# A three-block network on one core: the opening's first two weight units take the raw input, and their results are scaled afterwards

## The reference, cut to what matters

```python
def _rmsnorm(a, gain):
    af = a.astype(jnp.float32)
    af = af * lax.rsqrt(jnp.mean(af * af, axis=-1, keepdims=True) + EPS)
    return (af * gain.astype(jnp.float32)).astype(a.dtype)
...
    (q_sb, k_sb, v_sb, q_sp, k_sp, v_sp, q_ix, k_ix, w_ix,
     q_df, k_df, v_df, g_sb, g_sp, g_df) = _split_cols(u @ w_in)
...
        dots = jnp.einsum('bqjd,bkd->bqjk', qib.astype(jnp.float32), k_ixf)
        score = jnp.einsum('bqj,bqjk->bqk', wb.astype(jnp.float32), jax.nn.relu(dots))
        score = jnp.where((key_pos[None, :] <= qpos[:, None])[None], score, NEG_INF)
        _, sel = lax.top_k(score, top_k)
```

## Time and profile before

| | us |
|---|---|
| median of 3 runs | 2647.53 |
| lowest and highest of the runs | 2644.81, 2650.80 |
| the profiled execution | 2655.39 |
| its span, from the first instruction to the last | 2653.6 |

### The profile page before, as it was taken

The page is one execution under the profiler, slowest core; times in us unless marked ns, Lnnn a source line. Parts: engine busy times, 40 slices in busy tenths (PEclk is TensorE's granted clock), DMA queues, the critical chain, the costliest instruction groups (busy, mean ns, idle before and its releaser), DMA issues.

```text
span 2653.6 us, 36450 instructions
## 1 busy us (share of the span) xinstructions
PE 2548.8 (96%) x14788; PEld 2074.2 (78%) x14788; DVE 1481.2 (56%) x2440; ACT 1029.1 (39%) x1817; POOL 300.9 (11%) x213
## 2 busy tenths in 40 slices
PE   8889999999999999999999999999999999999998
PEld 6678898998998877766577777878866687788886
DVE  4987654554445457476547887454744644433444
ACT  4465454443223253235542223255333333322323
POOL 0143210012222010000012222020000000000001
PEclk9999999999999999998999999999999999999999
DMA  4211122223232341520035664332221132233332
GB/s 170 89 49 56 49 71 59 76 83 96 91 93 90 95 143 48 174 72 2 1 103 183 206 192 134 95 111 80 88 72 48 56 92 91 81 94 95 96 95 72
DMA packets 76980, 244.83 MB, mean 92 GB/s; under 512 B 12708, under 2 KB 18213, under 8 KB 76558
## 3 DMA queue, kind: packets, MB, share of 16 engines
q1 hardware_dynamic: 69470, 215.72, 26.3%
q10 hardware_dynamic: 7344, 26.77, 3.0%
HBM read 238.25 MB, written 6.90 MB: 92 GB/s over the span
## 4 chain that ended last, share of the span: by engine, by line
PE 66%; DVE 9%; ACT 3%; issue 2%; POOL 0%; DMA 0%; SPq 0%; ACTq 0%; DVEq 0%
PE ps L595 55%; DVE wl L379 2%; PE ps L2784 2%; ACT wh L367 1%; PE ps L1810 1%; PE ps L3477 1%; PE ps L1827 1%; PE ps L1838 1%; DVE xl L676 1%; DVE arena L1064 1%; DVE arena L3147 1%; PE ps L769 1%; PE ps L3461 1%; PE ps L1665 0%; PE ps L1545 0%
## 5 line engine op out<-in xcount | busy, mean ns | idle before, releaser
L595 PE MATMUL ps<-xh,wh 128*128 128x512 f32 (+1 forms) x2728 | 1006.7, 383 | 22.8 <-DVE xl L676 7.5
L595 PE MATMUL ps<-xl,wh 128*128 128x512 f32 (+1 forms) x2728 | 988.6, 377 | 0.0
L595 PE MATMUL ps<-xh,wl 128*128 128x512 f32 (+1 forms) x2728 | 984.4, 375 | 0.0
L379 DVE TENSOR_TENSOR wl<-ring,wh 128x1024 fp32r<-128x1024 f32 x374 | 472.8, 1264 | 593.8 <-ACT wh L367 593.0
L367 ACT ACTIVATE wh<-ring 128x1024 fp32r<-128x1024 f32 x372 | 393.2, 1057 | 938.9 <-PE ps L595 838.6
L595 PEld LDWEIGHTS ps<-xh,wh 128*128 128x128 f32 x2728 | 500.1, 189 | 151.3 <-issue 41.1
L595 PEld LDWEIGHTS ps<-xh,wl 128*128 128x128 f32 x2728 | 499.7, 189 | 97.8
L595 PEld LDWEIGHTS ps<-xl,wh 128*128 128x128 f32 x2728 | 498.3, 189 | 97.4 <-issue 5.5
L2060 PE MATMUL ps<-xh,wh 128*128 128x264 f32 (+1 forms) x816 | 254.2, 311 | 5.3 <-DVE xl L433 3.8
L759 POOL TENSOR_TENSOR arena<-arena 128x512 f32<-128x512 f32 (+1 forms) x35 | 60.2, 1726 | 1626.9 <-ACT arena L744 1626.9
L2060 PE MATMUL ps<-xl,wh 128*128 128x264 f32 (+1 forms) x816 | 233.3, 286 | 0.0
(11 more groups left out here) (388 smaller groups left out, 2571.1 us busy)
## 6 DMA issues: line engine op xcount, KB each, us to landing
ring<-in_weights SPq DMA_DIRECT2D x374, 512.0 KB, 3.6
arena<-in_w_ada ACTq DMA_DIRECT2D x48, 512.0 KB, 4.5
arena<-in_cmp_w SPq DMA_DIRECT2D x2, 2048.0 KB
strip_copies<-strip_scratch SPq DMA_DIRECT2D x8, 327.5 KB, 6.5
arena<-strip_copies SPq DMA_DIRECT2D x8, 264.0 KB, 4.0
out_features<-arena SPq DMA_DIRECT2D x8, 256.0 KB, 2.1
token_scratch<-arena SPq DMA_DIRECT2D x3, 512.0 KB, 6.8
arena<-token_scratch SPq DMA_DIRECT2D x12, 128.0 KB, 4.0
```

The costliest lines, as they stand in the source:

```text
L379: dve.tensor_tensor(flat(self.wl[:, s % 2]), flat(self.ring[:, s % RING]), flat(self.wh[:, s % 2]).bitcast(F32), ALU.subtract).then_inc(se ...
L595: last = pe.matmul(self.place(u, e), w[:, k, :], x[:, k, o:o + m], start=(k == 0 and i == 0), stop=(k == self.chunks - 1 and i == 2))
```

## The change

Units 0 and 1 now take the input times the gain, without the root. The new stages are:

- `raw`, an `Inputs` with gains: ACT rounds gain times chunk to `xh` straight from `h` (L616), DVE makes `xl` from `h`, gain and `xh` (L624).
- `RawSums`: ACT squares (L733); POOL adds squares 1 to 5 up (four additions, L746); PE sums square 0, the POOL's total, squares 6 and 7 with `ones` (L757), four pairs of products where there were eight; ACT makes the root (L737, L738).
- `Renormed`: the input is made once more, with gain and root (DVE L711, ACT L694, then the remainder L686, by POOL for chunks 2, 4 and 6, by DVE for the others), with three buffers where there were two. Unit 2 is the first to take it. Each chunk's `xh` waits until unit 1 has used the raw one (`raw_left`).
- `Scaled`: POOL multiplies the results of units 0 and 1 by the root (L775).

Unit 1 runs two chunks behind unit 0. The index keys become unit 0, the index queries units 1 and 2. ACT's queue now issues three of the four input transfers, and SP's issues the first unit's weights ahead of the fourth. The small work of `Prepare` moves from ahead of and within unit 2 to unit 3.

```diff
-    units = [pack_units(c) for c in [col[6], np.concatenate(col[7:9], 1)] + col[0:3] + col[9:12] + col[3:6]]
+    units = [pack_units(c) for c in [np.concatenate(col[7:9], 1), col[6]] + col[0:3] + col[9:12] + col[3:6]]
...
+class Renormed(Stage):
...
+        self.by_pool = (2, 4, 6)
...
+    def part(self, eng, k):
+        eng.wait_ge(self.hi.sem, self.hi.at(k + 1))
+        return eng.tensor_tensor(self.core.xl[:, k, 0:self.T], self.out[:, k % 3], self.core.xh[:, k, 0:self.T].bitcast(F32),
+                                 ALU.subtract)
...
+    def pool(self, pool):
+        for k in self.by_pool:
+            yield self.at + self.d * (k + 1) + 0.05
+            self.part(pool, k).then_inc(self.lo_pool.sem, 1)
+
+    def vector(self, dve):
+        for k in range(NC + 2):
+            yield self.at + self.d * k
+            if k == 0:
+                dve.wait_ge(self.sums.root.sem, self.sums.root.at(1))
+            if k >= 2 and k - 2 not in self.by_pool:
+                self.part(dve, k - 2).then_inc(self.lo.sem, 1)
+            if k < NC:
+                if k >= 3:
+                    self.split(dve, k - 3)
+                dve.scalar_tensor_tensor(out=self.out[:, k % 3], in0=self.tiles[k], scalar=self.gains[k], in1=self.sums.r,
+                                         op0=ALU.mult, op1=ALU.mult).then_inc(self.made.sem, 1)
...
+class RawSums(Stage):
...
+    def pool(self, pool):
+        for n in range(1, 5):
+            yield self.times[n + 1] + 0.1
+            pool.wait_ge(self.squared.sem, self.squared.at(n + 2))
+            if n > 1:
+                pool.wait_ge(self.added.sem, self.added.at(n - 1))
+            pool.tensor_tensor(self.acc, self.sq[:, 1] if n == 1 else self.acc, self.sq[:, (n + 1) % 4], ALU.add).then_inc(
+                self.added.sem, 1)
...
+class Scaled(Stage):
...
+    def pool(self, pool):
+        for n, a in enumerate(self.tiles):
+            yield self.at + 0.4 * n
+            pool.wait_ge(self.sums.root.sem, self.sums.root.at(1))
+            self.ready(pool, n)
+            pool.tensor_tensor(a, a, self.sums.r, ALU.mult).then_inc(self.done.sem, 1)
...
-        walk = [(u, e, k) for k in range(NC) for u in range(together) for e in range(2)]
+        walk, together, lag = [], 2 if self.x else 0, 2
+        for k in range(NC + lag if self.x else 0):
+            walk += [(0, e, k) for e in range(2) if k < NC] + [(1, e, k - lag) for e in range(2) if k >= lag]
...
-        for i in (1, 3):
-            self.load(sp, i)
+        yield -3.0
+        self.load(sp, 3)
...
-        for i in (0, 2):
+        for i in (0, 1, 2):
             self.load(act, i)
...
+    raw = Inputs(core, tokens_in, None, T, gains, landed, [-0.7, -0.66, -0.6, -0.54, -0.48, -0.44, -0.42, -0.4])
+    sums = RawSums(core, [-0.68, -0.64, -0.62, -0.58, -0.56, -0.52, -0.5, -0.46], tokens_in, landed, T, values + 5120, core.area(norm_tmp, T))
+    raw_left = core.take("raw_left", NC - 1)
+    core.chunk_used = [(raw_left.sem, raw_left.at(k + 1)) for k in range(NC - 1)] + [(core.used, 2)]
+    renormed = Renormed(core, tokens_in, 1.6, 0.125, T, sums, gains, norm_tmp + T)
```

More of the change, by code:

```diff
@@ L2874, in leave @@
         return act.activation(P1[:, u, o:o + n], got, ACT.Copy, scale=0.125 if u in (SB_Q, SB_Q + 1) else 1.0)
-    proj = Halved(core, N1, 0, halves(T), leave, x)
+    proj = Halved(core, N1, 0, halves(T), leave, (raw, renormed))
+    proj.raw_left = raw_left
+    scaled = Scaled(core, 2.2, [P1[:, u, :] for u in range(2)],
+                    lambda pool, u: pool.wait_ge(proj.free.sem, proj.free.at(2 * u + 2)), sums)
     whole = halves(T)
```

196 lines of the change are left out of this document (95 added, 101 removed).

## The result

The changed kernel takes **2658.28 us** (median of 7 runs, 2653.32 to 2662.75), beside 2647.53 for the kernel before (seven runs of each): a ratio of 1.0038 with a 95% interval of 1.0026 to 1.0050, so 6.9 to 13.2 us slower. The forecast was 2653.9, within 2645.0 to 2659.5: the median lies inside the range, 4.4 above the forecast.

A forecast was written before the change was run, and what follows sets the result against it. The opening's turning of the index weights was taken to set the end: root at 26.9, last chunk at 43.9, turning at 50.3 instead of 43.84. That 6.4 on the median 2647.53 gave 2653.9 us, range 2645.0 to 2659.5.

The forecast's parts named there:

- The first weights: Opening: the first unit's weights, issued at about 1.7, land at 7.7, with 7.4 and 10.07 as ends.
- Stops in the first part: Opening up to chunk 2: POOL's four additions each hold DVE 1.0, so chunk 2 is ready at 17.9 instead of 13.9.
- The root: Summed squares on TensorE, then logarithm, exponential and handing over: the root is there at 26.9, before it was 17.2.
- the low spell of 1.5: TensorE ahead of the root: one spell at 1.2 GHz, 15 products each 0.10 slower, adding 1.5 us.
- The second part: Root to last remainder: DVE's work 12.4 with waits, POOL's five operations holding it 4.6; last chunk ready at 43.9.
- From there to the turning: Last chunk to turning of the index weights: 3.3 for 27 products, 3.1 in unit 3; turning at 50.3, 6.4 later.
- rival 3: Weights still land at 10.07 and a second low-clock spell comes in unit 2: +7.4 to +9.5, about 2656; chance 0.15.
- Carried rigidly to the end: Behind the opening: what the turning of the index weights wins or loses reaches the kernel's end unchanged, here 6.4 us.
- Rival 1: Opening: POOL and DVE go side by side; turning at 40.4 to 43.3, 0.5 to 3.4 faster, about 2645.3; chance 0.15.
- Rival 2: Opening: POOL's operations meet DVE half as often, 4.3 less loss: +2, about 2649.6; chance 0.20.
- Rival 4: Opening: the second making of the input hides behind other TensorE work; faster by more than 5.3 us; chance 0.05.
- DVE's 12.1 behind the root: Root to last remainder: 8 norms, 5 remainders and `wl` of units 2 and 3 take DVE 12.1 us.

The follow-up runs named there:

- the run with clearings: Changed kernel with POOL's nine opening operations replaced by full-width clearings that read nothing, their computation left out: 2643.72 us, kernel before 2647.07.
- the run with filled gaps: Changed kernel with two unread products behind each of the first seven chunks of unit 2's first half, keeping TensorE busy: 2654.27 us, kernel before 2645.93.
- pool_silent: Changed kernel with POOL's nine opening operations replaced by one-column clearings, their computation left out: 2643.44 us, kernel before 2645.93.
- early_late: Changed kernel, TensorE summing all squares, norms starting with the root, all remainders on DVE, POOL's two multiplications behind the last remainder: 2640.69 us, kernel before 2647.07.
- early: Changed kernel, TensorE summing all squares, norms starting with the root, POOL keeping its three remainders: 2642.19 us, kernel before 2646.70.

## Why the prediction was right, and where its sizes were off

The direction and its cause were right: the turning later by the stops that POOL makes in DVE's list, and carried to the end. That the time fell within the range is not luck, but that the root was met so closely is, in part. Step by step:

- **The first weights** were taken to land so that DVE starts at 7.7; it started at 8.86, and between 8.33 and 8.94 in the twelve executions with this order of loads. The input transfer's own duration was the wrong likeness.
- **Stops in the first part**: forecast 4 of 1.0, measured 3.7 (cast +0.59, `wl` +0.97, the pair of raw remainders +2.11 against the run with clearings). That the cast would be held too is confirmed.
- **The root**: forecast 26.9, measured 26.4, by misses that cancel. The weights came 1.2 later than taken, chunk 2 0.4 late, and the low spell of 1.5 was hardly paid in this execution, since it fell on products that waited anyway. In the three other executions of this opening it was paid, and the root came at 28.0 to 28.4. The usual root lies 1.1 to 1.5 above the forecast.
- **The second part**: stops forecast 4.6, measured 0.61 + 1.05 + 1.03 + 1.09 + 1.10 = 4.9. The last remainder ended at 43.0, forecast 43.9.
- **From there to the turning**: forecast 6.4, measured 8.8. This is the step that was mis-sized in both executions of the change. It counted 27 and 12 products at 0.12, while TensorE stood at 1.2 GHz until 48. The prediction saw this as part of rival 3 ("a second spell of the low clock"), priced at 1.5 to 2, and left it out of the sum since no row of before had so broken a stretch; the run with filled gaps puts it at 2.5. With it the sum would have been +8.9 and 2656.4, against measured +8.88 and +10.75. The bursts that start slow, which the Trainium skill describes ("TensorE: Matmul & The Clock Gate", "HAM oscillation — how this bites in real kernels"), should have gone into the sum: the trace agrees in kind, 0.50 from 36 to 48, though here the level did not rise again between the chunks.
- **Carried rigidly to the end** held in thirteen comparisons, within 1.4 us in twelve of them.
- **Rival 1**, POOL beside DVE, named 40.4 to 43.3 and 2645.3: what pool_silent did, 41.10 and 2643.44. It was the right price for a wrong premise. **Rival 2**, half the meetings, didn't come: all nine meet. Of **rival 3** the first half didn't come (8.86, not 10.07), the second, the low spell, did. **Rival 4** took DVE's 12.1 behind the root as a floor, which gave 39.4; `early_late` turned at 38.11 with a root that rested on no addition of POOL. DVE's part behind the root was 13.0 even there, so the 12.1 was no bad floor; what was not one is the root at 20.9, which `early_late` had at 18.7.
- The warning that the profiled execution of before lay 7.9 above its median was heeded in the sum by adding only the difference; that its excess arose in one place, from 1150 to 1350 us, was not looked for.
- **Small slips of the working**, without effect on the sum: DVE's operation at 155.19 ends 0.56 after POOL's by the earlier trace rows, not 0.7, and the terms give rival 4 a root at 21.4 rather than 20.9 "at best".

## What to carry to other kernels

Work given to an idle GpSimd isn't free while VectorE runs two-input operations: ask what POOL reads and what stands in VectorE's list beside it, and charge VectorE with POOL's duration less some 0.3 us for each meeting, unless VectorE is waiting for something else in that time. Here, sums over chunks that TensorE took into its products with `ones`, early in its list, cost the path less, and POOL's unavoidable work belongs behind the last of VectorE's pieces that someone waits for. Where a term of waits for TensorE is added, add the low clock that follows it, and compare medians or one stretch of two traces, never two spans.

## What the runs showed of the hardware

- A GpSimd copy of 528 columns with one input stops a two-input VectorE operation by 0.3 to 0.4 us (1.12 for 0.70; 2.17 for two that met two copies, 1.44 alone), a two-input one mostly by 1.0 to 1.1 (1.80 for 0.70), a clearing of the same width not at all.
- Of a two-input operation on each engine the later one waits: beside POOL's multiplication `wl` took 2.34 where POOL had started 0.53 before it (`early`), and 1.22 where it had started 0.16 before POOL (`early_late`).
- The reverse: a clearing that began under VectorE's cast took 0.78 for 0.54.
- After its first waits TensorE's products came 0.22 apart while the clock column read 1.00 (in the four executions of the change's opening until 18.4, 22.1, 22.9 and 23.4 us). There the duration of the products tells the level, not the column.
- The same program has its root 2 us earlier or later by the moment at which that rate rises, 18.4 or 22 to 23 us. Its cause is open.
